# Sixteen more tokens of the last block go by gathered rows, and the gelu scratch shrinks to 336 tokens

## The chip, the cores and the metric

One core of a Trainium2 chip runs the whole layer. The metric is the device time of one execution in microseconds (us), as the median of a few executions. TensorE (PE) multiplies, VectorE (DVE), ScalarE (ACT) and GpSimd (POOL) compute, SyncE (SP) mostly issues DMAs; 16 DMA engines move the data.

## What is computed

A residual block on 512 tokens of width 1024, in float32: two kinds of attention and an output projection (with a LayerNorm), then a PEER layer, which the change is about:

```python
q = (xt @ w_q).reshape(T, PEER_HEADS, 2, half)            # 8 heads
s1 = einsum('thd,hnd->thn', q[:, :, 0], keys1)            # 128 keys each
s2 = einsum('thd,hnd->thn', q[:, :, 1], keys2)
v1, i1 = top_k(s1, 16); v2, i2 = top_k(s2, 16)
sc, pos = top_k(v1 + v2 over all pairs, 16)               # 128 experts a token
gate = softmax(sc)
a = einsum('nhkd,nd->nhk', u_tab[eidx], xb)               # rows of 1024
w = gelu(a) * gate
y = einsum('nhk,nhkd->nd', w, v_tab[eidx])
```

and x <- LayerNorm(alpha*x + y). There are 16,384 experts; u_tab and v_tab are 64 MB each.

## The kernel before

**Two ways for two kinds of tokens.** For the first 128 tokens the chosen rows of u_tab and v_tab are gathered, one row a partition (token) and call (`gather`, L793), and VectorE forms the dot products with x (`dot`, L1448) and the weighted sum (`add_row`). For the other 384 tokens the layer is dense: every expert's feature is computed by matmuls for all tokens, in 128 expert tiles of 128 experts, and the sum over experts runs over all of them with weights that are zero where an expert isn't chosen. Each fp32 operand is split in two fp32r parts, hi (ScalarE, L495) and lo (GpSimd or VectorE, L501), and three matmuls stand for one product.

**Late tokens.** The last 32 tokens of the last block are the exception: their features aren't computed by matmuls (so a feature matmul has 352 columns, `FEATURED`). Their 32 x 128 chosen rows are gathered as well, spread over all 128 partitions: 4 groups of 32 partitions, each with the same 32 tokens and another quarter of the ranks, so 32 gathers (`LATE_RANKS`) in place of 128. For that SyncE moves numbers, gates and x between partitions with 4 DMAs each (`move_numbers` L625, `move_gates` L632), and later the weights back (`move_weights` L639). The x that `dot` reads stands in PSUM (`x1_home`); ScalarE exchanges it for `late_x` and back (`home`), with VectorE waiting.

**Feature stage.** Expert tiles 0 to 43 run while VectorE does the routing (top-k by heads). Then come six rounds (`two_chunks`) of 12 tiles each, tiles 44 to 115, in which TensorE also scatters gates: in each round 8 groups of 8 tokens become a gate for each (expert, token), by products of one-hots that VectorE makes (`one_hots` L1672; four slots ahead) and that TensorE multiplies (`scatter` L2227) after certain tiles, the first after tile 46. ScalarE copies the result to `stage`, and SyncE stores it as g_scratch. For late tokens the weight (gelu times gate) is already known: it is turned by TensorE before the last round, split in three bf16 parts (`late_in_parts`) that lie in SBUF, and scattered in its last four groups by `late_hots` (L1702) and `late_scatter` (24 matmuls for 16), and the gelu of these tokens is taken as 1. Tiles 116 to 127 end the stage and stay in SBUF (`kept`); the gelu of the others goes through gelu_scratch in DRAM, with ones for the late tokens written once into the gelu buffers.

The order in each engine's program is written out by hand, each queue is in order, and semaphores connect them. GpSimd's program is a row of tiles: the split of a tile, then some gathers, each of which waits until VectorE has used the row before it in its slot (8 slots). It waits for `late_numbers_moved` before the split of tile 47. SyncE's program is the loads of the raw tiles, each waiting for a split four tiles back, with the moves between them.

**Combine stage.** 16 octets of 8 tiles: VectorE multiplies gelu (`ga`) and gates (`gg`, `gg8`) to a weight tile, ScalarE and VectorE split it, TensorE does 18 matmuls of 512 columns a tile. Beside it VectorE adds a gathered v row a tile. Of the first tokens' 128 u rows, 112 are dotted in the feature stage and 16 (`EXTRA`) in this one, one an octet and two in the first two octets (`extra_row`, `extra_dot_of` L1843).

## Time and profile before

| | |
|---|---|
| median of 3 runs | 1434.01 us (1432.75 to 1435.45) |
| profiled execution | 1433.48 us, span 1431.8 us, clock 0.997 |
| PE busy | 1406.7 us, 98% |
| DVE, ACT, POOL busy | 76%, 42%, 63% |
| moved by DMA | 415.41 MB, 290 GB/s over the span |

The span is from the first to the last instruction. PE's busy time is modelled at its ends, since matmuls overlap: the distance between starts tells more. A wait is named by the one that came last.

### The profile page before, as it was taken

The numbers are of one execution on the slowest core, as the hardware profiler recorded it, in microseconds if no ns is written. First come the engines' busy times: TensorE is split into PE (matmuls) and PEld (weight loads), VectorE is DVE, ScalarE is ACT, GpSimd is POOL, SyncE is SP. The second block draws the span as 40 slices with busy tenths as digits, with TensorE's granted clock in tenths as the row PEclk, the third lists the DMA queues.
The fourth block names the chain that finished last, engine by engine and source line by source line (L and its number), as shares of the span: only waits on it lengthen the run. The fifth ranks groups of instructions, "written<-read, shape, count | busy, mean of one in ns | idle before, by whom it ended". The sixth has DMA issues, their size and how long they took to land.

```text
span 1431.8 us, 24761 instructions
## 1 busy us (share of the span) xinstructions
PE 1406.7 (98%) x8045; PEld 1248.2 (87%) x8045; DVE 1087.3 (76%) x2324; ACT 606.7 (42%) x1019; POOL 903.4 (63%) x595
## 2 busy tenths in 40 slices
PE   9999999999999999999999999999999999999996
PEld 5888878888999999999999999878888888888885
DVE  5366666688999998858774885987777777777786
ACT  5666751324333354454544443333333333333332
POOL 3422331335599978979888786766666666666744
PEclk9999999999999999999999999999999999999998
DMA  6213120423689979999999899999999999999981
GB/s 243 75 50 113 59 90 1 147 84 102 197 316 342 323 259 395 417 389 418 418 417 399 341 381 407 383 388 387 371 374 374 372 366 360 367 368 366 372 315 59
DMA packets 138959, 415.41 MB, mean 290 GB/s; under 512 B 13904, under 2 KB 56656, under 8 KB 136720
## 3 DMA queue, kind: packets, MB, share of 16 engines
q1 hardware_dynamic: 80128, 240.69, 45.9%
q0 software_dynamic: 42064, 151.15, 26.8%
q10 hardware_dynamic: 16704, 22.81, 4.3%
q8 instruction: 29, 0.48, 0.1%
q14 instruction: 34, 0.28, 0.1%
HBM read 363.89 MB, written 50.14 MB: 289 GB/s over the span
## 4 chain that ended last, share of the span: by engine, by line
PE 76%; DVE 8%; DMA 5%; POOL 4%; issue 3%; ACT 2%; SPq 1%; DVEq 0%; ACTq 0%; POOLq 0%
PE banks L2019 12%; PE banks L2021 11%; PE banks L2020 11%; PE banks L1964 11%; PE banks L1965 11%; PE banks L1966 11%; DMA raw<-v_tab 3%; POOL lo L501 2%; PE banks L2081 2%; PE banks L2237 1%; PE banks L2238 1%; POOL rows L822 1%; PE banks L2174 1%; DMA rows<-u_rows,expert_at 1%; DVE rows L1454 1%
## 5 line engine op out<-in xcount | busy, mean ns | idle before, releaser
L501 POOL TENSOR_TENSOR lo<-raw,hi 128x1024 fp32r<-128x1024 f32 x224 | 540.2, 2413 | 416.5 <-ACT hi L495 396.5
L1964 PE MATMUL banks<-x1T_hi,hi 128*128 128x352 f32 (+3 forms) x1168 | 389.9, 334 | 1.3 <-ACT kept L1106 1.0
L1965 PE MATMUL banks<-x1T_lo,hi 128*128 128x352 f32 (+3 forms) x1168 | 384.6, 329 | 0.0
L1966 PE MATMUL banks<-x1T_hi,lo 128*128 128x352 f32 (+3 forms) x1168 | 383.6, 328 | 0.0
L495 ACT ACTIVATE hi<-raw 128x1024 fp32r<-128x1024 f32 x291 | 305.6, 1050 | 57.0 <-DMA raw<-u_t 37.4
L2019 PE MATMUL banks<-hi,wgt_hi 128*128 128x512 f32 x750 | 292.1, 389 | 2.0 <-DVE wgt_lo L1811 1.9
L2020 PE MATMUL banks<-lo,wgt_hi 128*128 128x512 f32 x750 | 291.8, 389 | 0.0
L2021 PE MATMUL banks<-hi,wgt_lo 128*128 128x512 f32 x750 | 291.8, 389 | 0.0
L1964 PEld LDWEIGHTS banks<-x1T_hi,hi 128*128 128x128 f32 x1168 | 219.8, 188 | 6.2 <-ACT kept L1106 1.3
L1966 PEld LDWEIGHTS banks<-x1T_hi,lo 128*128 128x128 f32 x1168 | 220.3, 189 | 4.4
L1965 PEld LDWEIGHTS banks<-x1T_lo,hi 128*128 128x128 f32 x1168 | 220.1, 188 | 3.9
L1454 DVE CUSTOM_DVE_ANT_0 rows<-rows,banks 128x1024 f32<-128x1024 f32 x144 | 172.5, 1215 | 61.0 <-DMA rows<-u_rows,expert_at 47.8
L1199 ACT ACTIVATE wgt_hi<-wgt 128x384 fp32r<-128x384 f32 x125 | 65.6, 525 | 313.1 <-PE banks L2021 284.4
L2019 PEld LDWEIGHTS banks<-hi,wgt_hi 128*128 128x128 f32 x750 | 140.8, 188 | 32.2 <-DVE wgt_lo L1811 2.7
L2021 PEld LDWEIGHTS banks<-hi,wgt_lo 128*128 128x128 f32 x750 | 140.8, 188 | 29.4
L2020 PEld LDWEIGHTS banks<-lo,wgt_hi 128*128 128x128 f32 x750 | 140.8, 188 | 29.2
L1860 DVE SCALAR_TENSOR_TENSOR banks<-rows,row_weight,banks 128x1024 f32<-128x1024 f32 x128 | 164.1, 1282 | 0.7
L822 POOL DMA_INDIRECT rows<-v_tab,expert_at x128 | 142.2, 1111 | 29.4 <-issue 21.1
L1811 DVE TENSOR_TENSOR wgt_lo<-wgt,wgt_hi 128x384 fp32r<-128x384 f32 x125 | 76.9, 616 | 108.6 <-ACT wgt_hi L1199 93.0
L822 POOL DMA_INDIRECT rows<-u_rows,expert_at x144 | 140.5, 975 | 28.8 <-issue 23.0
L1106 ACT ACTIVATE gelu<-banks 128x352 f32<-128x352 f32 x116 | 53.8, 464 | 241.4 <-PE banks L1966 229.1
L501 DVE TENSOR_TENSOR lo<-raw,hi 128x1024 fp32r<-128x1024 f32 x67 | 83.9, 1252 | 4.5 <-ACT hi L495 4.4
(245 smaller groups left out, 1846.7 us busy)
## 6 DMA issues: line engine op xcount, KB each, us to landing
raw<-u_t SPq DMA_DIRECT2D x128, 512.0 KB
raw<-v_tab SPq DMA_DIRECT2D x128, 512.0 KB
g_scratch<-stage SPq DMA_DIRECT2D x12, 2048.0 KB
gelu_scratch<-gelu ACTq DMA_DIRECT2D x116, 192.0 KB
ga<-gelu_scratch SPq DMA_DIRECT2D x29, 768.0 KB
gg<-g_scratch SPq DMA_DIRECT2D x14, 1536.0 KB
raw<-w SPq DMA_DIRECT2D x26, 512.0 KB
raw<-w_pq SPq DMA_DIRECT2D x16, 512.0 KB
```

What stands on the lines that cost most here:

```text
L495: act.activation(parts_of(c)[0][:, :], raw[:, c % RAW_SLOTS, :], ACT.Copy).then_inc(hi_ready, 1)
L501: eng.tensor_tensor(l[:, :], raw[:, c % RAW_SLOTS, :], h[:, :].bitcast(F32), ALU.subtract).then_inc(odd_lo_ready if by_vector(c) else lo_r ...
L822: pool.indirect_dma_start(rows[:, k % ROWS, :], None, table, at).then_inc(gathered[k % ROWS], 16)
L1454: dve.tensor_tensor_reduce(rows[:, k, :], rows[:, k, :], x1_home, 1.0, 0.0, ALU.mult, ALU.add, dots8[:, k:k + 1]).then_inc(row_used, 1)
L1811: dve.tensor_tensor(l[:, :], wgt[k % 2][:, :], h[:, :].bitcast(F32), ALU.subtract).then_inc(wgt_lo_ready, 1)
L1860: dve.scalar_tensor_tensor(y0, rows[:, k, :], row_weight[:, bass.ds(ROWS * r + k, 1)], y0, ALU.mult, ALU.add).then_inc(row_used, 1)
L1964: pe.matmul(o, h[:, s], hiT[:, k, tokens], start=(k == 0), stop=False)
L1965: pe.matmul(o, h[:, s], loT[:, k, tokens], start=False, stop=False)
L1966: ins = pe.matmul(o, l[:, s], hiT[:, k, tokens], start=False, stop=(k == KT - 1))
L2019: pe.matmul(o, h_at(b), h[:, s], start=start, stop=False)
L2020: pe.matmul(o, h_at(b), l[:, s], start=False, stop=False)
L2021: ins = pe.matmul(o, l_at(b), h[:, s], start=False, stop=stop)
```

## The change

Late tokens become 48: a set of 32 as before and a set of the 16 before them, which are spread over 8 groups of 16 partitions (16 gathers more, 48 in all). Feature matmuls have 336 columns. Each move of numbers, gates and weights is 12 DMAs instead of 4. The x in PSUM is exchanged once more: a second late x, moved by 8 DMAs into `sel`, is read by the dots of round 2, and the first tokens' x comes back at round 3. The feature stage keeps 144 gathers of u rows; so 32 of the first tokens' rows instead of 16 go to the combine stage, two an octet and three in octets 2 to 5, with a third buffer where the gelu buffers lie, and gelu and weight of these in two batches. In the last round the late groups are 2 to 7 instead of 4 to 7. The turn of the chosen numbers (`turn_chosen`) stands in tile 45 instead of 44. gelu_scratch holds 336 tokens; the ones are written once into `ga`, behind each tile's columns, and loads of `ga` fill four runs of 336.

```diff
-LATE_TOKENS = 32
-SPREAD = P // LATE_TOKENS
+LATE_SETS = (32, 16)
+LATE_TOKENS = sum(LATE_SETS)
...
-LATE_RANKS = RANKS // SPREAD
+LATE_RANKS = sum(RANKS // (P // n) for n in LATE_SETS)
+LATE_MOVES = sum(P // n for n in LATE_SETS)
...
-EXTRA = 16
+EXTRA = 32
+EXTRA_BATCHES = (16, 16)
...
+CHOSEN_AT = 1
+FIRST_BATCH_AT = 8
...
-    a_dram = nc.dram_tensor("gelu_scratch", (ETILES // 4, P, 4, DENSE), F32, kind="Internal").ap()
+    a_dram = nc.dram_tensor("gelu_scratch", (ETILES // 4, P, 4, FEATURED), F32, kind="Internal").ap()
...
-        gelu = [sb(f"gelu{i}", [P, DENSE]) for i in range(GELU_SLOTS)]
+        idle_gelu = ExitStack()
+        extra.append(sb("extra2", [P, D], F32, idle_gelu))
+        idle_gelu.close()
+        gelu = [sb(f"gelu{i}", [P, FEATURED]) for i in range(GELU_SLOTS)]
...
-        EXTRA_ASKED_AT, EXTRA_DOT_AT = (2, 4), (5, 7)
-        def extra_rows(j, par, at):
-            if isinstance(j, int) and j == 0:
-                return {k: (2 * par + i, i) for i, k in enumerate(at)}
-            return {at[1]: (2 * j + (2 + par), par)}
+        ASKED_AT = {2: (2, 4), 3: (0, 2, 4)}
+        DOT_AT = {2: (4, 6), 3: (2, 4, 6)}
+        def extra_number_of(i, each, q):
+            return (2 * i + (EXTRA_BATCHES[0] - 12 + q) if each == 2 else 3 * i + (q - 2)) if not early_extras(i) else 2 * i + q
+        def early_extras(i):
+            return isinstance(i, int) and i < 2
+        def late_sets():
+            first, column = P, 0
+            for n in LATE_SETS:
+                first -= n
+                for g in range(P // n):
+                    yield slice(first, first + n), slice(n * g, n * (g + 1)), slice(column, column + n)
+                column += n
...
-                for g in range(SPREAD):
-                    sp.dma_start(late_numbers[late_group(g), :],
-                                 block_numbers[LATE_AT:, late_group(g)]).then_inc(late_numbers_moved, 16)
+                for tokens, lanes, columns in late_sets():
+                    sp.dma_start(late_numbers[lanes, columns], block_numbers[tokens, lanes]).then_inc(late_numbers_moved, 16)
...
+            def move_second_x():
+                sp.wait_ge(selT_ready, 2)
+                for g in range(P // LATE_SETS[1]):
+                    sp.dma_start(late_x_second[LATE_SETS[1] * g:LATE_SETS[1] * (g + 1), :],
+                                 x1[LATE_AT:LATE_AT + LATE_SETS[1], TB - 1, :]).then_inc(late_x_moved, 16)
...
+                    if first and t == MID_TILES - 2:
+                        move_second_x()
...
-                            pool.wait_ge(late_numbers_moved, 16 * SPREAD)
+                            pool.wait_ge(late_numbers_moved, 16 * LATE_MOVES)
...
-            with pool.Fori(2, O_MID) as o:
+            some_rows((R_PRE + 4) * ROWS + AHEAD, 0, S_U + A_PRE + 2 * MID_TILES, 0)
+            with pool.Fori(3, O_MID) as o:
...
-            def v_octet(j, par):
...
+                    if k in ASKED_AT[each]:
+                        q = ASKED_AT[each].index(k)
+                        extra_number(extra_number_of(2 * j + par, each, q), q)
...
-            v_octet(0, 0)
-            v_octet(0, 1)
-            with pool.Fori(1, OCTETS // 2 - 1) as i:
-                v_octet(i, 0)
-                v_octet(i, 1)
+            v_octet(0, 0, 2)
+            v_octet(0, 1, 2)
+            for slot in range(GELU_SLOTS):
+                pool.wait_ge(gelu_stored[slot], 16 * (A_PRE + A_MID) // GELU_SLOTS)
+            with pool.Fori(1, 3) as i:
+                v_octet(i, 0, 3)
+                v_octet(i, 1, 3)
+            with pool.Fori(3, OCTETS // 2 - 1) as i:
+                v_octet(i, 0, 2)
+                v_octet(i, 1, 2)
...
+            def second_home():
+                act.wait_ge(late_x_moved, 16 * LATE_MOVES)
+                act.wait_ge(row_used, R_PRE * ROWS + LATE_SETS[0])
+                home(late_x_second)
...
-            def two_chunks(o, first=False, second=False, last=False):
+            def two_chunks(o, first=False, second=False, third=False, last=False):
...
-                        if first and tile == 0:
+                        if first and tile == CHOSEN_AT:
...
+                            second_home()
+                        if third and tile == 0:
...
-            for slot in range(GELU_SLOTS):
-                dve.memset(gelu[slot][:, FEATURED:DENSE], 1.0).then_inc(ones_ready, 1)
...
+            for slot in range(2):
+                dve.memset(ga[slot][:, :, FEATURED:DENSE], 1.0).then_inc(ones_ready, 1)
+            dve.wait_ge(ones_ready, 3)
...
-            def extra_dot_of(n, slot):
-                dve.wait_ge(extra_gathered[slot], 8 * (n - slot) + 16)
+            def extra_dot_of(n, slot, gathers):
...
-            def octet(j, par, made=0, split=0):
...
+                    if k in DOT_AT[each]:
+                        q = DOT_AT[each].index(k)
+                        n = extra_number_of(i, each, q)
+                        extra_dot_of(n, q, i + 1 if q < 2 else i - 1)
...
-            octet(0, 0, made=4, split=2)
-            octet(0, 1)
+                    if k in DOT_AT[each]:
+                        keep_extra_dot(n, q)
+            def weigh_extras(batch):
+                dve.wait_ge(dots_gelu_ready, 2 + batch)
+                weigh_rows(slice(FIRST_EXTRA + sum(EXTRA_BATCHES[:batch]),
+                                 FIRST_EXTRA + sum(EXTRA_BATCHES[:batch + 1]))).then_inc(row_weight_ready, 1)
+                dve.wait_ge(row_weight_ready, 2 + batch)
...
-                    if first and tile == 0:
+                    if first and tile == CHOSEN_AT:
...
-            pe.wait_ge(late_weight_moved, 16 * SPREAD)
+            pe.wait_ge(late_weight_moved, 16 * LATE_MOVES)
...

```

## Rows read from the trace of the kernel before

**Rows 1.** The page: busy time and share of each engine.

```profile
PE 1406.7 (98%) x8045; PEld 1248.2 (87%) x8045; DVE 1087.3 (76%) x2324; ACT 606.7 (42%) x1019; POOL 903.4 (63%) x595
```

**Rows 2.** Windows: stretch, length, busy us (instructions) of engines, PEclk, DMA share, GB/s.

```profile
650.00:700.00 50.00, 50.00 (x386) 48.96 (x385) 40.47 (x70) 22.58 (x37) 46.26 (x31) 1.00 1.03 420
...
928.40:960.80 32.40, 31.28 (x137) 25.22 (x135) 28.54 (x33) 11.84 (x16) 22.11 (x16) 1.00 1.01 397
...
1025.60:1058.00 32.40, 32.40 (x144) 26.84 (x143) 24.32 (x32) 11.82 (x16) 21.62 (x16) 1.00 0.99 369
```

**Rows 3.** Timeline of ACT (start, us, engine, line): gelu of two tiles.

```profile
846.28 0.46 ACT L1106 ACTIVATE gelu<-banks 128x352 f32<-128x352 f32 x1 [1.85 <-PE banks L1966]
...
850.12 0.46 ACT L1106 ACTIVATE kept<-banks 128x352 f32<-128x352 f32 x1 [2.43 <-PE banks L1966]
```

**Rows 4.** PE timeline: the first and the last of 13 matmuls, 384 columns.

```profile
243.22 0.33 PE L1964 MATMUL banks<-x1T_hi,hi 128*128 128x384 f32 x1
...
245.31 0.33 PE L1964 MATMUL banks<-x1T_hi,hi 128*128 128x384 f32 x1
```

**Rows 5.** Timeline of DVE: late numbers, and the end of the first one-hots.

```profile
519.75 0.23 DVE L1609 TENSOR_SCALAR row_weight<-dots_gelu 128x128 uint32<-128x128 f32 x1
...
530.85 0.68 DVE L1692 TENSOR_TENSOR gate_lo<-is_i,banks 128x1024 f16<-128x1024 f16 x1
```

**Rows 6.** Timeline of ACT: gelu of tile 46 and of tile 55.

```profile
532.58 0.46 ACT L1106 ACTIVATE gelu<-banks 128x352 f32<-128x352 f32 x1 [1.51 <-PE banks L1966]
...
574.93 0.46 ACT L1106 ACTIVATE gelu<-banks 128x352 f32<-128x352 f32 x1
```

**Rows 7.** SP timeline: a raw load, and the four moves of late numbers.

```profile
515.51 0.34 SPq L483 DMA_DIRECT2D raw<-u_t  x1
...
520.00 2.57 SPq L629 DMA_DIRECT2D small<-row_weight  x4
```

**Rows 8.** Timeline of POOL: copy of late numbers, and the split of tile 56.

```profile
523.86 0.19 POOL L815 COPY expert_at<-small 128x8 uint32<-128x8 uint32 x1 [4.29 <-DMA small<-row_weight]
...
570.43 2.41 POOL L501 TENSOR_TENSOR lo<-raw,hi 128x1024 fp32r<-128x1024 f32 x1
```

**Rows 9.** Timeline of DVE: the late weights parts, idle before them.

```profile
791.92 0.20 DVE L1739 CAST row_weight<-small 128x64 bf16<-128x64 f32 x1 [17.14 <-ACT small L1192]
```

**Rows 10.** Groups by line and form, DVE, 505 to 860 (count | busy, mean).

```profile
L1688 DVE TENSOR_TENSOR is_i<-banks,selT 128x1024 f16<-128x1024 f16 x88 | 56.6, 685 | 3.3 <-PE banks L2238 2.4 <-issue 0.6
...
L1692 DVE TENSOR_TENSOR gate_lo<-is_i,banks 128x1024 f16<-128x1024 f16 x44 | 30.0, 681 | 0.0
...
L1692 DVE TENSOR_TENSOR gate_hi<-is_i,banks 128x1024 f16<-128x1024 f16 x44 | 29.8, 678 | 0.0
...
L1721 DVE TENSOR_TENSOR gate_lo<-is_i,row_weight 128x1024 bf16<-128x1024 bf16 x6 | 10.3, 1710 | 0.0
...
L1721 DVE TENSOR_TENSOR gate_hi<-is_i,row_weight 128x1024 bf16<-128x1024 bf16 x6 | 8.3, 1383 | 0.0
...
L1717 DVE TENSOR_TENSOR is_i<-banks,selT 128x1024 bf16<-128x1024 f16 x8 | 5.1, 681 | 0.0
```

**Rows 11.** ACT timeline: gelu of two tiles, a late group between them.

```profile
821.40 0.46 ACT L1106 ACTIVATE gelu<-banks 128x352 f32<-128x352 f32 x1 [2.07 <-PE banks L1966]
...
826.67 0.46 ACT L1106 ACTIVATE gelu<-banks 128x352 f32<-128x352 f32 x1 [2.89 <-PE banks L1966]
```

**Rows 12.** The chain that ended last, in order of time: start, us, what.

```profile
869.93 4.52 SPq L483
```

**Rows 13.** DVE and ACT timelines: low part of a weight, high of the next.

```profile
900.58 0.55 DVE L1811 TENSOR_TENSOR wgt_lo<-wgt,wgt_hi 128x384 fp32r<-128x384 f32 x1
...
901.90 0.53 ACT L1199 ACTIVATE wgt_hi<-wgt 128x384 fp32r<-128x384 f32 x1 [2.60 <-PE banks L2021]
```

**Rows 14.** Timelines of POOL and DVE: an extra row's gather, and its dot.

```profile
1201.22 0.94 POOL L864 DMA_INDIRECT extra<-u_rows,small  x1 [0.30 <-issue]
...
1213.45 2.34 DVE L1848 CUSTOM_DVE_ANT_0 extra<-extra,x 128x1024 f32<-128x1024 f32 x1
```

More of the change, by code:

```diff
@@ L1187, in _ @@
             two_chunks(2, second=True)
-            with act.Fori(3, O_MID - 1) as o:
+            two_chunks(3, third=True)
+            with act.Fori(4, O_MID - 1) as o:
                 two_chunks(o)
@@ L1750, in _, with two_chunks @@
             one_hots(0, 0, True)
-            def two_chunks(o, first=False, second=False, last=False):
+            def two_chunks(o, homes=None, first=False, last=False):
                 for tile in range(8):
@@ L1868, in _, with octet @@
             dve.wait_ge(residual_ready, 1)
-            def octet(j, par, made=0, split=0):
+            def octet(j, par, each, made=0, split=0):
                 i = 2 * j + par
-                extras = extra_rows(j, par, EXTRA_DOT_AT)
                 for k in range(8):
@@ L2257, in two_chunks @@
                     at = tile % 4, 3 * o + (A_PRE // 4 + tile // 4)
-                    if first and tile == 0:
+                    if first and tile == CHOSEN_AT:
                         turn_chosen(at)
```

114 lines of the change are left out of this document (62 added, 52 removed).

## The prediction

> **What bounds the kernel now.** I read the busy shares first, then stages, then the order of time around the places where TensorE meets another engine. TensorE is busy 98% of a span of 1431.8 us [rows 1], so a cut in its columns looks like pure gain. But its neighbours are nearly full too: in the middle of the feature stage the 16 DMA engines show a share of 1.03 and GpSimd is busy 46 of 50 us, in the first octets of the combine stage DMA is at 1.01 and TensorE loses 1.1 of 32.4 us, and in a quiet octet DMA is still at 0.99 [rows 2]. So the question is how much of the time that TensorE gives up is in stretches where nothing else is late.
>
> **What is removed: 16 columns of each feature matmul.** ScalarE takes up an expert tile when its 24 matmuls end, and two such starts are 3.84 us apart [rows 3], 160.0 ns a matmul at 352 columns. At 384 columns twelve matmuls take 245.31 - 243.22 = 2.09 us [rows 4], 174 ns. That is 0.44 ns a column, near the 0.417 ns of one column a cycle at 2.4 GHz, the clock level of these rows (PEclk 1.00, [rows 2]). 336 columns should take 160.0 - 16 x 0.417 = 153.3 ns, a tile 3.68 us. 128 tiles x 0.16 = 20.5 us is the most that this part can bring. The Trainium skill ("TensorE: Matmul & The Clock Gate", Back-to-back issue gap) gives a sustained spacing of about 81 ns at 128 columns and 131 ns at 512, both operations of a pair included. By that slope, 0.13 ns a column, a matmul would give back 2.1 ns and the part at most 6.4 us; the rows, which are fp32r, speak against it, and I use the rows.
>
> **Before tile 46: the gain is lost to VectorE.** The routing on VectorE doesn't depend on TensorE's speed here. It ends with the last block's numbers at 519.75, and the first group's one-hots end at 530.85 + 0.68 = 531.5 [rows 5]. The first scatter stands after tile 46, whose matmuls ended at 532.6 [rows 6]. Its cover is thus 1.1 us. TensorE would be there 47 x 0.16 = 7.5 us sooner and can use 1.1. Moving the turn of the chosen numbers by one tile takes away the stall on gates_ready (7 us earlier TensorE would stand there), but not this one: DVE's order up to the one-hots is the same. What was saved is worth 1.1 us at tile 47.
>
> **The moves on SyncE: the next gate.** Late numbers are moved by 4 DMAs, now by 12. The four issues begin at 520.00 and take 2.57 us [rows 7], 0.64 each; GpSimd, which waits for all of them before it splits tile 47, is released at 523.86 after 4.29 us of idling [rows 8]. Eight more issues, each of half the partitions: from above the 0.64 each of the same moves, 5.1 us; from below the 0.34 of a raw load's issue at 515.51 [rows 7], 2.7 us. I take 0.6 each, near the same kind, 4.8 us. Behind this wait GpSimd runs without a pause of more than 0.3 us until tile 56, split at 570.43 + 2.41 = 572.84 [rows 8]; TensorE starts tile 56 at 574.93 [rows 6]. The cover is 2.1 us, so tile 56 starts at 572.84 + 4.8 = 577.6, that is 2.7 us later than before (0.6 to 3.0), and the 1.1 us of tile 47 is gone as well. Queued behind the 12 issues on SyncE are the loads of tile 50 and of those behind it; tile 50 is split five gathers and three splits after tile 47, so they stay covered. The same moves of the gates (behind tile 55's load) and of the weights (after the fourth round), and the 8 of the second x (4.8 us before tile 63's load), delay one u load each by 2 to 4 us. I cost them at nothing: a split that is late by so much has the 2.1 us of cover found above, and a load has the splits queued ahead of it besides; if that cover is gone it is about 1 us each.
>
> **Rounds to the last.** From tile 57 to tile 103 TensorE sets the pace: 47 x 0.16 = 7.5 us gained. One more exchange of the x in PSUM (ScalarE copies, VectorE's dots wait for it, GpSimd's gathers wait for the dots) has the form of the one that exists, which costs TensorE nothing (in 650 to 700, just behind it, it is busy 50.00 of 50 us, [rows 2]); cost nothing. DMA must carry the same gathers in 3.5% less time, at a share already 1.03 [rows 2]; bytes fall a little (each gelu store by an eighth), so I count it as just enough. Balance at the start of the last round: 2.7 - 7.5 = **-4.8 us** (-6.9 to -4.5).
>
> **The last round and the change of stage.** VectorE enters the last round on time: it has waited 17.14 us for the turned weights, which come from TensorE [rows 9]. From there it does one group after another, and two more groups become late ones. A usual group takes (56.6 + 30.0 + 29.8) / 44 = 2.65 us, a late one (10.3 + 8.3 + 5.1) / 4 = 5.92 [rows 10]; two more are +6.5 us. What makes them dear is in the same rows: a product with its factor in PSUM takes 0.68 us, one with its factor in SBUF 1.4 to 1.7 on average, and the change only moves the parts from one SBUF tensor to another. TensorE in the same round gains 12 x 0.16 = 1.9 and loses 2 x 0.45 = 0.9 (a late group has 24 matmuls for 16: tiles end 826.67 - 821.40 = 5.27 us apart with a late group between them, [rows 11], against 3.84 + 16 x 0.056 = 4.8). Six late groups in a row, beside VectorE's dots, leave little of its lead of one-hots; I expect TensorE to wait 1 to 3 us for them, inside the sum below. GpSimd's gathers wait for VectorE's dots, and its splits are behind them in order, so the 6.5 us are passed on. At the end of the features the chain that ended last goes from an odd tile split by VectorE to the load of the last u tile at 869.93 [rows 12] and to the v tiles behind it. Cover: the low part of the third combine weight is ready at 900.58 + 0.55 = 901.1, and TensorE is through with the tile before it at 901.9, where it releases ScalarE [rows 13]: 0.8 us. So the combine stage starts 6.5 - 0.8 = 5.7 us later than before, counted from the start of the last round, and not 2.9 us earlier (24 x 0.16 - 0.9). I take **+5.7**; ends -2.9 (all of it beside DMA that is late anyway) and +6.5.
>
> **The combine stage.** Here TensorE does what it did. Added: 16 gathers, 16 dots, two each octet instead of one and three in octets 2 to 5; the dot of the last one comes 2 tiles after its gather instead of 3. A gather was issued at 1201.22 and its dot began at 1213.45, 12.2 us on; the dot takes 2.34 us [rows 14]. One tile less leaves 9.3 us and 1.5 us of cover behind it. VectorE has 24.3 of 32.4 us filled [rows 2] and bears two more dots. DMA: 524,288 bytes at the octet's 369 GB/s is 1.4 us of its time. An octet with two more rows needs 0.99 x 32.4 + 2.8 = 34.9, less 0.5 for the two shorter gelu loads, is 34.4 us at share 1.00, 33.1 at 1.04, which such stretches reach: 0.7 us over TensorE's 32.4, four times, 2.8; the four tiles of parts held ahead take about half. The others need 33.0 at 1.00, 31.7 at 1.04: nothing. I take **+1.3 us** (0 to +8: 34.4 - 32.4 four times). The gelu pieces now land as four runs of 1344 B in place of one of 6144 B a partition; at that length I cost it at nothing (1 us either way). The ones: four small memsets at the routing's start go and two come before the first weights; some tenths of a us at most. The second batch of gelu and weights is two small operations.
>
> **Sum.** -4.8 + 5.7 + 1.3 = +2.2 us on the profiled execution's 1433.48 us (span 1431.8 and 1.7 around it): 1435.7, and as the median of the three runs shown (1434.01) is 0.5 above that execution but within their spread, I say **1435.5**. The case's own range is 1430 to 1440. A change of under 0.2%, 2.9 us, can't be told from none.
>
> **Rivals.**
> A, *the lateness drowns in DMA.* At the change of stage DMA is full (1.01 still at 928 to 961, [rows 2]) and rows are awaited for it, so VectorE's 6.5 us may be waited out by loads that are late anyway. Then the 2.9 us stay gained: -4.8 - 2.9 + 0 = -7.7, 1426. For it: TensorE lost only 1.1 us in that octet [rows 2]. Against: the chain of waits goes over VectorE through the whole last round.
> B, *DMA becomes the bound of the combine stage*, slower. Place: octets 2 to 5 and their raw v loads; price: 34.4 - 32.4 = 2.0 us each, +8 in place of +1.3; it decides from the point where the share can't exceed 1.00. -4.8 + 5.7 + 8 = +8.9, 1442. For it: TensorE stalled at 397 GB/s and 1.01. Against: 420 GB/s at 1.03 in the feature stage. The Trainium skill ("DMA: Bandwidth & Descriptors", Where 436 GB/s comes from) puts the fabric at 435 GB/s and HBM at about 358 a core; the trace has 420, so the second doesn't bind here, and the first leaves 4%.
> C, *the gates give way*: routing and moves follow TensorE, and all of the columns count, -20.5 + 1.3: 1414. Against: nothing in [rows 5, 7] waits for TensorE.
>
> **Chances.** Forecast 0.46, A 0.27, B 0.21, C 0.06. Range for 8 in 10: 1425 to 1442, which takes in A and most of B. Faster by over 0.2%: A, C and 0.02 of the forecast, 0.35. Slower: B and 0.14 of the forecast, 0.35. Within: 0.30.
>
> **What would show it.** Feature tiles 3.68 us apart; the first scatter still near 531 to 532; GpSimd released for tile 47 near 528.7; TensorE idle some 11 us before the second round, about 6 of them for the turn and the first scatter and 5 for low parts at tiles 49 to 56; the last round 4 to 7 us nearer to the start of the span; VectorE 6 us longer in it; TensorE waiting for one-hots and, at 870 to 960, for low parts. Wrong if SyncE's issues of 16 rows are far cheaper (then 2 us better), if tiles of the late round never wait, or if octets 2 to 5 last over 34 us.

## The result: 1.8% slower, and the profile after

The changed kernel takes 1458.74 us (median of 4 runs, 1457.20 to 1461.83) against 1433.71 for the kernel before (4 runs): the ratio is 1.0176, interval 1.0155 to 1.0196. Forecast were 1435.5 us and a range of 1425 to 1442. The profiled execution has a span of 1460.1 us against 1431.8, 28.3 us more. Those 28.3 us are laid out below.

The page's busy times, the line that answers to [rows 1]:

```profile
PE 1413.7 (97%) x8061; PEld 1236.5 (85%) x8061; DVE 1102.3 (75%) x2373; ACT 608.0 (42%) x1021; POOL 922.5 (63%) x627
```

TensorE has 128 x 24 x 16 columns less to do and is busy 7 us **more**. No wait explains a longer busy time. Either instructions take longer or the clock is lower, and here it is both. I cut the time by events that both traces have: the gelu of a tile, and the high part of combine weights (w8 is the tenth of the 128 that ScalarE makes, w124 the 126th, with 116 tiles between them). ScalarE's timeline in the changed kernel, tiles 46, 47, 56, 62 and 103, then w8 and w124:

```profile
530.23 0.45 ACT L1141 ACTIVATE gelu<-banks 128x336 f32<-128x336 f32 x1 [1.36 <-PE banks L2031]
540.37 0.45 ACT L1141 ACTIVATE gelu<-banks 128x336 f32<-128x336 f32 x1 [3.99 <-PE banks L2031]
...
586.71 0.43 ACT L1141 ACTIVATE gelu<-banks 128x336 f32<-128x336 f32 x1
...
618.75 0.45 ACT L1141 ACTIVATE gelu<-banks 128x336 f32<-128x336 f32 x1 [0.18 <-PE banks L2031]
...
799.17 0.45 ACT L1141 ACTIVATE gelu<-banks 128x336 f32<-128x336 f32 x1
...
942.15 0.53 ACT L1241 ACTIVATE wgt_hi<-wgt 128x384 fp32r<-128x384 f32 x1 [2.73 <-PE banks L2086]
...
1428.19 0.51 ACT L1241 ACTIVATE late_hi<-wgt 128x384 fp32r<-128x384 f32 x1
```

The same events in every kernel that is discussed here (us, each from the profiled execution; the last column is the median of its runs):

| kernel | tile 0 at | 0-46 | 46-62 | 62-103 | 103-w8 | w8-w124 | median |
|---|---|---|---|---|---|---|---|
| before | 353.3 | 179.3 | 73.1 | 184.7 | 137.9 | 472.5 | 1433.7 |
| changed | 355.0 | 175.3 | 88.5 | 180.4 | 143.0 | 486.0 | 1458.7 |
| pad | 353.3 | 175.2 | 88.0 | 179.8 | 143.6 | 479.4 | 1453.8 |
| numbers_apart | 353.3 | 175.3 | 84.6 | 179.0 | 144.0 | 477.3 | 1448.3 |
| spread | 355.0 | 175.2 | 82.8 | 181.1 | 144.8 | 476.4 | 1446.0 |
| spread_mixed | 353.4 | 175.2 | 85.2 | 178.7 | 143.7 | 472.3 | 1442.6 |
| no_second_x | 352.7 | 175.1 | 80.6 | 178.2 | 143.7 | 473.3 | 1437.1 |
| act_moves | 353.3 | 175.2 | 79.8 | 181.3 | 142.9 | 470.0 | 1437.4 |
| act_moves_back | 352.8 | 179.8 | 74.7 | 185.0 | 141.0 | 477.2 | 1442.4 |
| columns_only | 355.2 | 180.3 | 72.5 | 178.0 | 139.5 | 470.0 | 1427.0 |
| columns_back | 353.3 | 179.1 | 84.3 | 185.1 | 141.1 | 478.9 | 1456.1 |
| odd_dots | 354.5 | 175.2 | 88.1 | 178.7 | 144.3 | 476.5 | 1449.9 |

So the 28.3 us are +1.7 ahead of tile 0, -4.0 to tile 46, **+15.4 between tiles 46 and 62**, -4.3 to tile 103, +5.1 over the last round and the change of stage, **+13.5 in the combine stage** and +0.9 behind it. The first is no part of the change: other executions, the unchanged stages of columns_only among them, show it too (a granted clock of 0.91 from 250 to 270).

**Tiles 46 to 62: the queue.** SyncE's queue, and what GpSimd waited for, answering to [rows 7, 8]:

```profile
521.71 9.15 SPq L650 DMA_DIRECT2D small<-row_weight  x12
...
557.07 8.30 SPq L656 DMA_DIRECT2D small<-sel  x12
...
589.64 5.60 SPq L662 DMA_DIRECT2D sel<-x  x8
595.29 2.77 SPq L495 DMA_DIRECT2D raw<-u_t  x1
598.11 1.10 SPq L682 DMA_DIRECT2D g_scratch<-stage  x1
```
```profile
532.15 0.19 POOL L843 COPY expert_at<-small 128x8 uint32<-128x8 uint32 x1 [14.31 <-DMA small<-row_weight]
```

Twelve moves hold the queue 9.15 us, and GpSimd is released at 532.15 in place of 523.86. The u load that stands behind the 8 moves of the second x is issued at 595.29; the split that frees its slot had ended at 593.05. ScalarE's timeline from there, with what it waits for:

```profile
594.90 0.45 ACT L1141 ACTIVATE gelu<-banks 128x336 f32<-128x336 f32 x1
596.28 1.06 ACT L507 ACTIVATE hi<-raw 128x1024 fp32r<-128x1024 f32 x1 [0.93 <-DMA raw<-u_t]
...
598.58 0.45 ACT L1141 ACTIVATE gelu<-banks 128x336 f32<-128x336 f32 x1 [1.23 <-issue]
606.03 1.06 ACT L507 ACTIVATE hi<-raw 128x1024 fp32r<-128x1024 f32 x1 [7.00 <-DMA raw<-u_t]
...
615.01 1.06 ACT L507 ACTIVATE hi<-raw 128x1024 fp32r<-128x1024 f32 x1 [6.61 <-DMA raw<-u_t]
```

The 7.00 us before 606.03 are the wait for that load. The 6.61 us before 615.01 are for the next one, issued at 599.25 behind a store of 2048 KB of gates. That second wait isn't the moves': columns_only, which has none of them, waits nearly as long for a load behind the same store, with TensorE busy 9.93 of the 10 us from 600:

```profile
604.52 1.06 ACT L495 ACTIVATE hi<-raw 128x1024 fp32r<-128x1024 f32 x1 [6.32 <-DMA raw<-u_t]
```

Behind the first of the two TensorE waits 4.42 us, to 607.63, its longest wait of the stage. The chain that ended last passes through the same load, though up to 588 it runs over VectorE's dots and one-hots and over gathered rows; in order of time, start, us and what:

```profile
594.49 0.80 POOL rows L850
595.29 10.72 DMA raw<-u_t
```

**And the clock.** Windows of TensorE around the first scatter and around tile 60 (length, busy us (instructions), granted clock, DMA share, GB/s):

```profile
525.00:530.00 5.00, 5.00 (x34) 1.00 0.13 38
530.00:535.00 5.00, 1.34 (x19) 0.98 0.32 106
535.00:540.00 5.00, 5.00 (x23) 0.68 0.91 304
600.00:605.00 5.00, 3.21 (x21) 1.00 1.02 355
605.00:610.00 5.00, 2.37 (x19) 0.65 1.07 452
610.00:615.00 5.00, 5.00 (x24) 0.67 0.97 397
```

And what that looks like in TensorE's timeline:

```profile
534.91 0.62 PE L2029 MATMUL banks<-x1T_hi,hi 128*128 128x336 f32 x1 [2.31 <-POOL lo L513]
535.33 0.48 PE L2030 MATMUL banks<-x1T_lo,hi 128*128 128x336 f32 x1
535.61 0.48 PE L2031 MATMUL banks<-x1T_hi,lo 128*128 128x336 f32 x1
535.89 0.48 PE L2029 MATMUL banks<-x1T_hi,hi 128*128 128x336 f32 x1
```

Behind the two waits at the scatter (1.35 and 2.31 us) matmuls start 0.28 us apart, 336 columns at the 1.2 GHz level, against 0.153 at 2.4. Such a stall is paid twice: once idle, once slow. With 0.32 to 0.35 of the clock missing over 5 and over 10 us that is at most 1.6 and 3.4 us; part of the second falls into the wait that lasts to 607.63. The kernel before has 1.00 throughout this stage. In columns_back, with the 16 columns back and all else as in pad, the clock doesn't fall at the scatter (1.00 from 530 to 540) but still falls at tile 60 (0.70 from 600 to 610). Nor does it fall at the scatter in numbers_apart and act_moves (1.00 from 530 to 540), which keep the cut and release GpSimd by 526: the cut alone doesn't bring the first fall, the late numbers beside it do (in spread a wait of 3.43 us for the one-hots does the same, 0.66 from 530 to 540). The second fall is that of the late load: it stays in numbers_apart (0.66 from 600 to 610) and is gone in act_moves (1.00). Not every long wait is followed by a fall. In spread TensorE waits 3.10 us, to 588.54, and its windows there are:

```profile
585.00:590.00 5.00, 1.90 (x22) 1.00 1.05 380
590.00:595.00 5.00, 5.00 (x35) 1.00 1.04 397
```

**The combine stage: a longer matmul.** TensorE's timeline, two matmuls 20 steps apart, first of the kernel before, then of the changed one:

```profile
1099.72 0.39 PE L2019 MATMUL banks<-hi,wgt_hi 128*128 128x512 f32 x1
...
1104.25 0.39 PE L2021 MATMUL banks<-hi,wgt_lo 128*128 128x512 f32 x1
```
```profile
1119.75 0.40 PE L2084 MATMUL banks<-hi,wgt_hi 128*128 128x512 f32 x1
...
1124.42 0.40 PE L2086 MATMUL banks<-hi,wgt_lo 128*128 128x512 f32 x1
```

4.53 / 20 = 226.5 ns before, 4.67 / 20 = 233.5 after, with no idle time between them, and a window that answers to the last of [rows 2] has 140 matmuls in 32.40 us for 144, at a clock of 1.00:

```profile
1120.00:1152.40 32.40, 32.40 (x140) 26.08 (x139) 23.70 (x33) 10.72 (x17) 22.13 (x17) 1.00 1.01 383
```

Seven ns for each of the 2088 matmuls between w8 and w124 are 14 us. Their program is the same. What is not the same is where their weights lie: shorter gelu buffers and a wider `small` move everything behind them by 640 bytes.

### The profile page after: what moved, and what is told of

It reads as the page before. It is cut to its first block, busy times and chain, and to the rows that moved or that the text cites. A ratio compares the mean times of both kernels' runs of the same rounds, so it can differ in the third digit from the quotient of the medians.

```text
span 1460.1 us, 24627 instructions
## 1 busy us (share of the span) xinstructions
PE 1413.7 (97%) x8061; PEld 1236.5 (85%) x8061; DVE 1102.3 (75%) x2373; ACT 608.0 (42%) x1021; POOL 922.5 (63%) x627
## 4 chain that ended last, share of the span: by engine, by line
PE 53%; DVE 19%; DMA 10%; issue 8%; POOL 5%; ACT 2%; SPq 1%; DVEq 0%; POOLq 0%; ACTq 0%
PE banks L2084 12%; PE banks L2085 12%; PE banks L2086 12%; PE banks L2029 4%; DMA rows<-u_rows,expert_at 4%; PE banks L2031 4%; PE banks L2030 4%; POOL lo L513 3%; DVE rows L1504 3%; DMA raw<-u_t 2%; PE banks L2146 2%; POOL rows L850 2%; DMA extra<-u_rows,small 1%; DVE sel L1639 1%; DVE is_i L1738 1%
## 5 line engine op out<-in xcount | busy, mean ns | idle before, releaser
L2029 PE MATMUL banks<-x1T_hi,hi 128*128 128x336 f32 (+3 forms) x1168 | 386.3, 331 | 11.3 <-POOL lo L513 7.8
L2030 PE MATMUL banks<-x1T_lo,hi 128*128 128x336 f32 (+3 forms) x1168 | 379.0, 324 | 0.0
L2031 PE MATMUL banks<-x1T_hi,lo 128*128 128x336 f32 (+3 forms) x1168 | 378.6, 324 | 0.0
L2084 PE MATMUL banks<-hi,wgt_hi 128*128 128x512 f32 x750 | 296.4, 395 | 2.7 <-DVE wgt_lo L1860 2.7
L2086 PE MATMUL banks<-hi,wgt_lo 128*128 128x512 f32 x750 | 296.2, 395 | 0.0
L2085 PE MATMUL banks<-lo,wgt_hi 128*128 128x512 f32 x750 | 296.2, 395 | 0.0
L850 POOL DMA_INDIRECT rows<-v_tab,expert_at x128 | 136.5, 1066 | 29.5 <-issue 23.5
L1141 ACT ACTIVATE gelu<-banks 128x336 f32<-128x336 f32 x116 | 52.3, 451 | 189.1 <-PE banks L2031 173.8
L513 DVE TENSOR_TENSOR lo<-raw,hi 128x1024 fp32r<-128x1024 f32 x67 | 87.6, 1307 | 5.8 <-ACT hi L507 5.8
```

Source lines behind the costliest of these rows:

```text
L513: eng.tensor_tensor(l[:, :], raw[:, c % RAW_SLOTS, :], h[:, :].bitcast(F32), ALU.subtract).then_inc(odd_lo_ready if by_vector(c) else lo_r ...
L850: pool.indirect_dma_start(rows[:, k % ROWS, :], None, table, at).then_inc(gathered[k % ROWS], 16)
L2029: pe.matmul(o, h[:, s], hiT[:, k, tokens], start=(k == 0), stop=False)
L2030: pe.matmul(o, h[:, s], loT[:, k, tokens], start=False, stop=False)
L2031: ins = pe.matmul(o, l[:, s], hiT[:, k, tokens], start=False, stop=(k == KT - 1))
L2084: pe.matmul(o, h_at(b), h[:, s], start=start, stop=False)
```

## Experiments

All medians are shown with that of the kernel before on the same chip, as its ratio.

**1 and 2. The address, undone and alone.** pad:

```
-        small = sb("small", [P, P + 32])
+        small = sb("small", [P, P + 64])
```

> The changed kernel with one edit: the tensor `small` is 64 columns wider than before the change instead of 32, so that the combine weights' parts behind it start 512 bytes earlier than in the kernel before instead of 640 (214016, a multiple of 512, where the changed kernel has 213888 and the kernel before 214528). Theory L (address): a combine matmul took 226.7 ns before and takes 233.3 ns in the changed kernel because its 128x128 weights cross a 512-byte line; here it takes 226.7 again, 2250 of them and 36 of the late parts give back 2286 x 6.7 ns = 15.2 us, time 1458.7 - 15.2 = 1443.5. Rival D (contention): more gathers and more DMA writes slow the reads; the matmul stays at 233.3 and the time at 1458.7. Nothing else moves.

Measured 1453.77, ratio 1.0123 (1.0092 to 1.0155) for 1.0176. The matmul is back at 226.5 ns, as the address says. TensorE's timeline, 20 steps:

```profile
1119.80 0.39 PE L2084 MATMUL banks<-hi,wgt_hi 128*128 128x512 f32 x1
...
1124.33 0.39 PE L2086 MATMUL banks<-hi,wgt_lo 128*128 128x512 f32 x1
```

But w8 to w124 lost only 6.6 us of the 14, and the median 5: something else stood right behind it (experiment 5). before_shift is the kernel before with the same kind of edit:

```
-        small = sb("small", [P, P])
+        small = sb("small", [P, P + 32])
```

> The kernel before with one edit: `small` is 32 columns (128 bytes) wider, nothing else. Theory L: the combine weights' parts now start at 214656, 128 bytes past a multiple of 512, each 128x128 block crosses a line, a combine matmul takes 233.3 ns in place of 226.7, and the time is 1433.7 + 15.2 = 1448.9. Rival D: no more gathers and no more DMA than before, so 226.7 ns and 1433.7.

Measured 1444.51, ratio 1.0070 (1.0045 to 1.0095), 10 us slower for 128 unused bytes. Its matmuls, 19 steps, are 232.1 ns apart (4.41 / 19):

```profile
1099.84 0.39 PE L2021 MATMUL banks<-hi,wgt_lo 128*128 128x512 f32 x1
...
1104.25 0.40 PE L2019 MATMUL banks<-hi,wgt_hi 128*128 128x512 f32 x1
```

The same matmuls on the same data, with no change in gathers or DMA: the address does it, and contention is out. I expected 15 us. Of the 5 us less 2.5 are a step of 232.1 and not 233.3 (2088 x 1.2 ns), and 1.8 are waits of the kernel before that the slower matmuls cover: from w8 to w16 it takes 33.7 us, before_shift 31.9. Which multiple counts was asked of one more kernel (`P + 64`, 256 bytes):

> The kernel before with `small` 64 columns (256 bytes) wider, so that each 128x128 block of the combine weights starts 256 bytes past a multiple of 512. If what counts is that a block (512 bytes a partition) lies on a 512-byte line, a combine matmul takes 233.3 ns as with a shift of 128; if it is the multiple of 256, 226.7 as before. The time follows: about 1445 or 1434.

One run, 1432.62. Matmuls are 227.0 ns apart:

```profile
1099.76 0.39 PE L2020 MATMUL banks<-lo,wgt_hi 128*128 128x512 f32 x1
...
1104.30 0.39 PE L2019 MATMUL banks<-hi,wgt_hi 128*128 128x512 f32 x1
```

So my 512-byte line was wrong. Weights 0 or 256 bytes past a multiple of 512 are fast, at 128 (before_shift) and 384 (changed) they are slow: of the offsets tried, the multiples of 256 are the fast ones. Others were not tried. Over all steps from w8 to w124 the means are 226.7 ns before, 233.3 changed, 226.8 in pad, 232.4 in before_shift and 226.7 in before_shift_256.

**3. Part of the change alone: scratch and ones.** Gelu buffers and scratch of 352 tokens, ones put into `ga`, on the kernel before:

> The kernel before with one part of the change alone: gelu buffers and gelu scratch hold the 352 tokens of the feature matmuls, and ones stand behind each tile's columns in the two sum buffers. Late tokens 32, as before. All behind the gelu buffers moves by 4 x 32 x 4 = 512 bytes, so under theory L the combine weights stay on a line: 226.7 ns a matmul. Expected by me: no change, 1433.7 within 1.5 (the loads of the gelu pieces come as four runs a partition). Rival: these shorter runs cost DMA time in the first octets and the last round, 2 to 4 us slower.

Measured 1434.77, ratio 0.9998 (0.9983 to 1.0013). The shorter runs and the moved ones cost nothing, and the 512 bytes that the buffers give up keep the weights on a multiple of 256. The changed kernel's gelu buffers give up 768 and `small` takes back 128, and that breaks it.

**4. The moves.** spread is pad with this on SyncE (and a semaphore of its own for the second set's numbers, so that GpSimd waits for 4 moves at tile 47):

```
-                for tokens, lanes, columns in late_sets():
+                for tokens, lanes, columns in list(late_sets())[:FIRST_MOVES]:
                     sp.dma_start(late_numbers[lanes, columns], ...)
...
-                    if first and t == 3:
-                        move_gates()
-                    if first and t == MID_TILES - 2:
-                        move_second_x()
+                    if isinstance(o, int) and (o > 0 or t >= 2):
+                        for _ in range(MOVES_EACH):
+                            next(between, None)
```

> `small` as in the padded kernel, and the moves on SyncE's queue apart: of the numbers' 12 moves only the first set's 4 stand before tile 47; the second set's 8, the 8 of the second x and the 12 of the gates are issued two behind each load from the third load of the first round on, and GpSimd waits for the second set's numbers only at the first row that needs them. Theory Q (the queue): SyncE's 9.15 us of numbers' moves, 8.3 of the gates' and 5.6 of the second x are what made GpSimd 6.6 us late at tile 47 and the loads late at tiles 55, 60 and 61; with them apart tile 62's gelu is near its time in the kernel before (605.7) less a few us, instead of 13 us behind, and the time is 12 to 15 us under the padded kernel's, some 1430. Rival R (DMA): the stage is bound by the bytes and packets of the DMA engines (share 1.03), the stalls come back at the next tiles, and the time is within 3 us of the padded kernel's, some 1442.

Measured 1446.01, ratio 1.0065 (1.0030 to 1.0099): 8 us off, less than the 12 to 15 expected. The stretch 46-62 falls from 88.0 to 82.8, where before has 73.1. numbers_apart delays the second set's numbers only:

```
-                for tokens, lanes, columns in late_sets():
+                for tokens, lanes, columns in list(late_sets())[:FIRST_MOVES]:
                     sp.dma_start(late_numbers[lanes, columns], ...)
+            def second_numbers():
+                for tokens, lanes, columns in list(late_sets())[FIRST_MOVES:]:
+                    sp.dma_start(late_numbers[lanes, columns], ...).then_inc(second_numbers_moved, 16)
+                    yield
...
+                    if first and t >= 4:
+                        next(numbers, None)
```

> The padded kernel (1453.8) with one edit: of the numbers' 12 moves the second set's 8 come one behind each load from tile 56's on, and GpSimd waits for them only at the first row that needs them; the gates' 12 and the second x's 8 stay where the change has them. Theory Q1 (the 9.15 us in front of tile 47 are the cause): GpSimd is released 6 us sooner, tile 62 comes some 6 us sooner (610), 1447. Theory Q2 (the loads' queue is the cause, and the first moves are only its first stop): the gates' 8.3 us and the second x's 5.6 us hold the loads as before, tile 62 comes 1 to 2 us sooner (615), 1452.

1448.25, ratio 1.0106 (1.0086 to 1.0125). GpSimd is released at 525.33, 4.7 us sooner than in pad (530.07):

```profile
525.33 0.91 POOL L857 COPY expert_at<-small 128x8 uint32<-128x8 uint32 x1 [9.21 <-DMA small<-row_weight]
```

Of those 4.7 us 3.4 are left at tile 62 (613.1 against 616.5), between the two theories. act_moves then takes the other 28 moves off SyncE altogether (with the dots of experiment 5):

```
+            def moves_between():
+                act.wait_ge(late_numbers_ready, 1)
+                for tokens, lanes, columns in list(late_sets())[FIRST_MOVES:]:
+                    act.dma_start(late_numbers[lanes, columns], ...).then_inc(second_numbers_moved, 16)
+                    yield
...
                         gelu_tile(tile % 4, 3 * o + (A_PRE // 4 + tile // 4))
+                        if isinstance(o, int) and (o > 0 or tile >= 3):
+                            for _ in range(MOVES_EACH):
+                                next(between, None)
```

> As the kernel with the moves apart and mixed dots, but the second set's numbers (8 moves), the second x (8) and the gates (12) are issued from ScalarE's queue, two behind each tile's gelu from tile 47 on; only the first set's 4 stay on SyncE. Theory Q (a load waits behind the moves in SyncE's queue and in its ring): tile 62 comes 4 to 5 us sooner than with the moves on SyncE, near the 606 of the kernel that has only the narrower matmuls, and the time is some 1434. Rival R (the bytes and the DMA engines decide, whoever issues): no change, 1438 to 1439.

1437.43, ratio 1.0022 (1.0007 to 1.0037), where the same kernel with the moves on SyncE (spread_mixed) has 1442.6. Tile 62 comes at 608.3 instead of 613.8. no_second_x leaves the second x's 8 moves out instead (16 tokens are then computed from another x):

> As the kernel with the moves apart and mixed dots, without the 8 moves of the second x; the 16 rows' dots of the second set then use another x, so these 16 tokens are computed from wrong data. It leaves out 512 KB of transfers between tiles 53 and 58 and 8 issues. With the moves apart TensorE still came 5.2 us later to tile 62 than with the narrower matmuls alone, 3.3 of it at tiles 55 to 58. Theory R: these bytes, 1.2 us at 420 GB/s and up to 3 us with their latency on the loads' ring, are most of it: 3 to 4 us sooner at tile 62, 1435. Rival: they are not, and it is the gates' moves and the store of the first gates beside them: tile 62 moves less than 1 us, 1438.

1437.07, ratio 1.0028 (1.0015 to 1.0040), the same time as with all of the moves on ScalarE's queue. Tile 62 is 5.4 us sooner than in spread_mixed. Issuing the moves elsewhere does as well as not moving the 512 KB, which speaks for their place in front of a load as the cause and against their bytes. It isn't shown cleanly: act_moves takes 20 other moves off SyncE's queue too, and the second x alone on another queue was not run. The 2048 KB store in front of a load shows that bytes in the same queue do count. ScalarE bears two moves in 1.15 us between its own pieces:

```profile
556.51 1.06 ACT L510 ACTIVATE hi<-raw 128x1024 fp32r<-128x1024 f32 x1
...
557.08 1.15 ACTq L1200 DMA_DIRECT2D sel<-x  x2
558.28 1.09 ACT L1175 ACTIVATE stage<-banks 128x512 f32<-128x512 f32 x2 [0.71 <-issue]
```

**5. The extra rows' dots.** In pad TensorE waits for the low part in the octets from the sixth on. VectorE's timeline there:

```profile
1214.77 1.27 DVE L513 TENSOR_TENSOR lo<-raw,hi 128x1024 fp32r<-128x1024 f32 x1
1216.65 1.23 DVE L1900 CUSTOM_DVE_ANT_0 extra<-extra,x 128x1024 f32<-128x1024 f32 x1 [0.61 <-DMA extra<-u_rows,small]
...
1217.80 2.75 DVE L1860 TENSOR_TENSOR wgt_lo<-wgt,wgt_hi 128x384 fp32r<-128x384 f32 x1
```

The dot stands in a tile with a split, in front of that tile's low part, and the low part itself takes 2.75 us instead of 0.55. In the combine stage such a low part takes over 1.2 us 16 times in pad and 4 times in the kernel before. GpSimd's timeline tells what these have in common:

```profile
1217.72 2.42 POOL L513 TENSOR_TENSOR lo<-raw,hi 128x1024 fp32r<-128x1024 f32 x1 [2.00 <-ACT hi L507]
```

All 20 overlap a split on GpSimd and end 0.41 to 0.42 us after it (here the split ends at 1220.14 and the low part at 1220.55). The dots behave alike: 1.2 us clear of a split, and in the kernel before 14 of 16 take about 2.3 us and end 1.1 us after one (the 2.34 of [rows 14] among them). A dot in front of a low part decides whether the low part meets a split. TensorE, waiting:

```profile
1220.60 0.50 PE L2084 MATMUL banks<-hi,wgt_hi 128*128 128x512 f32 x1 [0.40 <-DVE wgt_lo L1860]
```

odd_dots:

```
-        DOT_AT = {2: (4, 6), 3: (2, 4, 6)}
+        DOT_AT = {2: (5, 7), 3: (3, 5, 7)}
```

> The padded kernel with one edit: VectorE's dots of the extra rows stand at tiles 5 and 7 of an octet (3, 5 and 7 in octets 2 to 5), where VectorE has no split of a v tile, instead of 4 and 6 (2, 4 and 6), where it has one. Theory V (VectorE's crowded tile): weight 0.55, row 1.28, split 1.22, dot 1.22 and the low part 0.56 are 4.8 us in a tile of 4.08, so TensorE waits 0.4 to 0.8 for the low part at such tiles and the octet takes 33.7 instead of 32.6; with the dots at odd tiles the octets from 6 on take 32.7, some 5 us less in all, 1449. Rival B (DMA is the bound of the combine stage, 34.4 us of transfers an octet): no change, 1453.8.

1449.86, ratio 1.0099 (1.0078 to 1.0121). The nine octets and a half from w48 to w124 take 308.2 us, as before (308.4), where pad has 314.2 (the 316.0 of a later expectation was a miscount; 314.2 it is). With one extra row more an octet, this stretch costs nothing. From w16 to w48 it takes 137.3, against 132.5 in pad. So spread_mixed keeps the change's places there, `{2: (5, 7), 3: (2, 4, 6)}`:

> The kernel with the moves apart and `small` padded (1446.0) with the extra rows' dots at tiles 5 and 7 in octets with two of them, and at 2, 4 and 6, where the change has them, in octets 2 to 5 with three. With all dots at odd tiles, octets 6 to 15 took what they took before (308.2 us for the last 76 tiles with weights against 308.4 before and 316.0 in the padded kernel) but octets 2 to 5 took 137.3 for 32 tiles against 132.5. Theory V: both gains stay, so 316.0 - 308.3 = 7.7 us off, 1438 to 1439. Rival B (DMA bound): what is not waited for at one place is waited for at the next, 1444 to 1446.

1442.60, ratio 1.0066 (1.0045 to 1.0087), against 1446.01: 3.4 us for 7.7 expected. w8 to w124 takes 472.3, the 472.5 of before. The 137 us in w16 to w48 came back in act_moves_back (137.8), with the mixed dots, so the odd places can't be its only cause. The traces show low parts of the same kind there. In act_moves_back a dot waits for its row before one:

```profile
980.35 1.23 DVE L1910 CUSTOM_DVE_ANT_0 extra<-extra,x 128x1024 f32<-128x1024 f32 x1 [3.35 <-DMA extra<-u_rows,small]
...
981.50 2.69 DVE L1870 TENSOR_TENSOR wgt_lo<-wgt,wgt_hi 128x384 fp32r<-128x384 f32 x1
```

TensorE then waits 3.53 us for it, and 1.06 and 0.39 for two more of 2.73 and 2.79 us; in odd_dots it waits 0.36, 1.16, 0.81 and 1.60. Why the row was late in the one kernel and not in act_moves stays open.

**6. The cut, alone and undone.** columns_only is the kernel before with `tokens=slice(P, SEQ - LATE_TOKENS - 16)`, nothing added (the features of 16 tokens are left out):

> The kernel before with the feature matmuls 16 columns narrower (336 for 352) and nothing else; the features of 16 tokens are left out, so this shows what the cut alone can bring with no work added for it. Theory N (the neighbours decide): of 20.5 us of columns the part before tile 46 turns into a wait for VectorE's one-hots, which with no cover left comes with a fall of the granted clock behind it; loads and splits hold the tiles up to 62; from tile 63 on 0.16 us a tile count, 65 x 0.16 = 10.4, less what DMA takes back at the change of stage. Time 1423 to 1428, that is 6 to 11 us faster. Rival C (TensorE decides): 1434.6 - 20.5 = 1414.

1426.96, ratio 0.9944 (0.9922 to 0.9966). A cut of 20.5 us of TensorE's work, with no work added for it, brings 7. Its row in the table says where: from tile 0 to tile 62 252.8 us against 252.4, nothing at all; then 184.7 - 178.0 = 6.7, all of 41 tiles' columns; then +1.6 at the change of stage and -2.5 in the combine stage. Up to tile 62 TensorE waits for the neighbours, and its clock falls behind the wait:

```profile
510.00:520.00 10.00, 7.63 (x48) 1.00 0.75 254
520.00:530.00 10.00, 8.43 (x47) 0.83 0.25 64
530.00:540.00 10.00, 10.00 (x78) 1.00 0.97 340
```

columns_back is pad with `tokens=slice(P, SEQ - LATE_TOKENS + 16)`:

> The padded kernel (combine weights on a 512-byte line again) with the 16 columns put back: the feature matmuls have 352 columns, of which 336 are used; all the moves, gathers, late groups and extra rows of the change stay. Theory N: the columns were worth little, for TensorE waits where it has them less, so the time is 3 to 8 us above the padded kernel's (1453.8), 1457 to 1462, and the clock falls less between tiles 47 and 62. Rival C: 1453.8 + 20.5 = 1474. If it is below 1455, the cut was worth nothing in this surrounding.

1456.08, ratio 1.0165 (1.0125 to 1.0204), 2.3 us above pad: by the ratios it is 6 us, and the two intervals overlap. Beside the moves in SyncE's queue the cut was worth little, and how much isn't clear of the noise. act_moves_back is the same edit on act_moves:

> The kernel with the moves on ScalarE's queue and mixed dots (1437.4) with feature matmuls of 352 columns, of which 336 are used. In the padded kernel the same edit cost 2.3 us, and in the kernel before the opposite one brought 7. If the columns are worth something as soon as the additions are off the loads' queue, 1437.4 + 7 = 1444; if the neighbours (VectorE's one-hots, GpSimd's splits, DMA at the change of stage) still take what TensorE gains, 1437 to 1440.

1442.39, ratio 1.0053 (1.0036 to 1.0071), 5.0 us above act_moves, between the two expectations. With the additions off the loads' queue the cut is worth 5 to 7 us, and they cost 8 to 9 (act_moves_back against before, by the ratio and by the medians), 3.1 of them in the last round and the change of stage.

**7. The turn's place.** turn_44 is spread with `CHOSEN_AT = 0`, act_turn_44 the same on act_moves:

> The kernel with the moves apart and `small` padded (1446.0), with the turn of the chosen numbers back at tile 44. The change's place for it, tile 45, leaves one wait of 3.4 us at the first scatter, behind which the feature matmuls took 280 ns (the lower clock level, 336 columns at 1.2 GHz) for 3.4 us. Theory K (one long wait brings the clock down, two short ones don't): TensorE waits about 1.9 us for the gates before tile 44's turn and 2 us at the scatter, its clock stays up, 1.5 to 2 us gained: 1444. Rival: the wait is as long or the clock falls as well, 1446 or above.

> As the kernel with the moves on ScalarE's queue and mixed dots (1437.4), with the turn of the chosen numbers at tile 44 in place of 45. With the moves on SyncE it made no difference (1447.6 against 1446.0). If the turn's place only decides where TensorE waits, 1437.4 again; if it decides whether the wait at the first scatter brings the clock down, 1 to 3 us either way.

1447.59 against 1446.01 and 1438.11 against 1437.43: no difference clear of the noise in either. Theory K's two short waits did not come: in turn_44 TensorE waits 3.93 us once, at the turn (to 520.86), and the clock is at 0.83 from 520 to 530, behind that wait in place of behind the scatter. act_turn_44 has the same 0.83 there, where act_moves has no fall, and is as fast.

No version of the whole change beats the kernel before. The nearest, act_moves, is 0.2% slower. The medians on the way there are 1458.7, 1453.8 with the address mended, 1446.0 with the moves apart, 1442.6 with the dots' places and 1437.4 with the moves on ScalarE's queue.

## Why the prediction was wrong, step by step

- **"The columns": right.** 3.68 us a tile was expected and is there (from tile 62 to 103, 180.4 us against 184.7, and 178.0 in columns_only). The sustained figures of the Trainium skill ("TensorE: Matmul & The Clock Gate", Back-to-back issue gap) would have it, by their slope, at 2.1 ns a matmul in place of 6.7; the 336 columns started 153 ns apart (3.68 us from 594.90 to 598.58, by 24), so for these fp32r matmuls the rows decide against them and for the 1/2.4 ns a column of the same section's formula for an isolated matmul. "Before tile 46 the gain is lost to VectorE" was right in kind: the first scatter waited 1.35 us for the one-hots. That it began at 531.54, within the forecast 531 to 532, is luck, for this execution is 1.7 us late; in pad it began at 529.7.
- **"The moves on SyncE", first gate: mis-sized.** 8 more issues at 0.6 were 4.8 us. The 0.6 was near (the gates' twelve take 8.30, 0.69 each), but these eight were 6.6 (9.15 - 2.57), of which one issue alone took 2.25 us, and the numbers themselves came 1.7 later (521.45 for 519.75), as all of that execution. I had 528.7 for GpSimd's release, it was 532.15.
- **"I cost them at nothing": the first step that failed.** The gates' 12 and the second x's 8 moves were to be covered by 2.1 us. This cover I had already spent on the numbers' moves. They stood 8.3 and 5.6 us in front of loads in a stretch whose DMA share is about 1.0. ScalarE waited 5.04 us (to 571.59) and 7.00 us (to 606.03) for the raw tiles right behind them, and TensorE 4.42 us behind the second. I forecast the start of the last round 4.8 us earlier; it came 8.8 later, of which 1.7 are not the change's. Moving them to another queue (act_moves) brings back 5.2 us of median against spread_mixed, leaving the second x out 5.5.
- **No step for the clock: missing.** Two of the waits, at the scatter and at tile 60, were followed by 5 to 10 us at a granted 0.65 to 0.68. That is up to 5.0 us between 535 and 615, as much as I had for all of the moves. The idle time ahead of the second round was near the forecast, 10.1 us (355 to 587) for "some 11"; the 4.42 us at tile 60 come on top.
- **"The last round and the change of stage": right in sum.** +5.7 forecast, 143.0 - 137.9 = +5.1 measured from tile 103 to w8. Its parts were not: without the cut the additions cost 3.2 there (columns_back), and the cut alone gives not 2.9 back but costs 1.6 (columns_only). That the sum agrees is luck.
- **"In the combine stage TensorE does what it did": the second step that failed.** +1.3 forecast, +13.5 measured. I looked at what the change does to the work and not at what it does to the layout: 640 bytes less in front of the weights, and each of their matmuls is 7 ns longer. pad and before_shift show it from both sides.
- **"VectorE has 24.3 of 32.4 us filled and bears two more dots": wrong by the mean.** The octet had room, the tile that the dot was put in had not, and a low part that meets a split on GpSimd takes up to 2.8 us in place of 0.55, which no mean shows. The 2.34 us of a dot were of the same kind: clear of a split it takes 1.2. In the changed kernel this was hidden by the slower matmuls; with the address mended it is 5.8 us from w48 on, and in odd_dots it is gone.
- **Rivals.** A (lateness drowns in DMA) and C (the gates give way) did not come. B had a stall in the combine stage (+8 for +13.5, or +6.9 with the address mended), for the wrong reason: DMA is not its bound, for the same 16 gathers more fit into 472.3 us with the dots elsewhere. All four cases were about waits. None was about the length of an instruction.

## What to carry to other kernels

Where an engine is cut that its neighbours keep up with only just, price the cut by stretches: here the first 62 of 128 tiles gave nothing, and the reserve that went with them turned each late transfer into a wait and then into slow matmuls. Small DMAs belong on a queue in which nothing urgent stands behind them, however few their bytes: the gates' twelve are of 1 and 4 KB. And when a change alters the size of any on-chip buffer, list the addresses behind it before and after: the weights of matmuls should keep their alignment, and a pad of some bytes is a free test of it.

## What the runs showed of the hardware

- A 128 x 128 fp32r matmul with 512 moving columns took 226.5 to 227 ns with its weights at a multiple of 256 bytes in the partition and 232 to 233.5 ns at 128 bytes past one, with no idle time and nothing else changed. Of these matmuls' operands only the weights moved: the moving one lies ahead of `small`. Other instructions on the shifted buffers kept their times (the high part of a weight 525 ns before and 526 after).
- Some waits of TensorE of 2.3 to 4.4 us were followed by stretches at a granted clock of 0.65 to 0.83, with matmuls of 336 columns 280 ns apart in place of 153; others were not (3.10 us in spread, to 588.54, at 1.00).
- VectorE's subtraction of two 128x384 tensors in SBUF took 0.55 us, but 1.26 to 2.79 us in the 16 cases in pad (and 4 in the kernel before) that overlapped a split on GpSimd; all ended 0.41 to 0.42 us after that split.
- The issue of a move of 16 partitions was no cheaper on SyncE's queue than one of 32: 0.70 each for the eight of the second x (16 partitions), 0.69 for the gates' twelve of both sizes, against 0.64 for the four of 32 in the kernel before; single ones took longer (2.25 us at 522.29). On ScalarE's queue two took 1.15 to 1.2 us.
